# Expert stage of a hybrid transformer layer: gate by tanh, token rows stored already modulated, and the low parts of gate/up weights on VectorE

## The chip, the cores and the metric

The kernel runs on one core of one Trainium2 chip. The metric is device time in microseconds, the median of the runs. The core's engines are TensorE (PE in the profile; PEld is its weight load), VectorE (DVE), ScalarE (ACT), GpSimd (POOL) and SyncE (SP), which issues most of the DMAs. Each engine works through its own list in order, and lists meet only at semaphores.

## What is computed

One layer on 2048 tokens of width 1024, in float32: a mixer (attention and retention), then an expert-choice feed-forward. What matters here is the part behind the mixer:

```python
x = x + ga1 * y                                     # y: mixer output @ w_o
h = rmsnorm(x, g_norm_ffn) * (1.0 + sc2) + sh2
aff = jax.nn.softmax(h @ w_router, axis=-1)         # 16 experts
g, idx = lax.top_k(aff.T, 256)                      # each expert picks 256 tokens
xs = h[idx]
a, u = xs @ w_gate, xs @ w_up                       # 1024 -> 768, per expert
out = (silu(a) * u) @ w_down * g                    # 768 -> 1024
x = x + ga2 * scatter_add(out, idx)
return rmsnorm(x, g_final)
```

## The kernel before

The stages run one behind the other. TensorE multiplies in a fast 32-bit form that keeps fewer bits than float32, so each large operand is split in two: ScalarE rounds it (the high part), VectorE or GpSimd subtract that from the whole (the low part, or "rest"), and three products high x high, high x low, low x high are added up (`PASSES`). The low part overwrites the whole, in place.

**First stage** (`modulation`): the products that give shift and scale. `perm["modcols"]` holds them as columns, columns 24 to 31 the feed-forward's shift, 32 to 39 its scale, into which `g_norm_ffn` is folded last (`s_fold`). At its end SyncE stores one row (`scratch["ga2"]`), waits for that, and goes on to load the first tile of x for the projection stage.

**Output stage** (`mix_out`): one turn per tile m of 128 tokens, 16 turns. TensorE makes the first half of y(m) (24 products of 512 columns), transposes the normed rows of tile m-1 (8 transposes, L1289), makes the second half of y(m), and the router product of m-1 (L1297). VectorE multiplies y by ga1 (L1384), adds x (L1386); ScalarE squares, takes a logarithm and an exponential (L1331 to L1336, each of the two behind a table load), which gives the inverse root; VectorE scales (`xn`, L1392). `xn`, not yet modulated, is stored to `scratch["xn2"]` and transposed. After the transposes VectorE applies scale and shift to the transposed tile, two instructions for each half (L1359, L1361), for the router. GpSimd makes the low parts of the mix tiles (L1269).

**Expert stage** (`experts`): one turn per expert e, 16 turns. TensorE's list of a turn:

- six gate/up pieces f = 0 to 5 (`gate_up`, L1614), 48 products each of 256 columns, 24 for gate and 24 for up; piece f uses the weights of group c = f // 2. Behind f = 1 it makes the slot table of expert e+1.
- two groups of four transposes of e+1's gathered rows (T0 and T1, `transposes`, L1600), into banks 6 and 7.
- twelve down pieces i = 0 to 11 (`down`, L1628), six products of 512 columns each, with T2 behind piece 2 (bank 6 again) and T3 behind piece 3 (bank 7 again).

Each piece f gives a gate in `ex` (ScalarE, Exp), then VectorE's `hidden` in four steps (add 1, reciprocal, two products), ScalarE's rounding and VectorE's low part (L1852). The gathered rows go from the bank by VectorE's `modulate` (L1818 from the bank, L1820 in place), ScalarE's `round_gathered` (L1665) and VectorE's `rest_gathered` (L1826). T2 and T3 wait for `modulated`: the first modulate step of the group two back.

Weights: SyncE loads gate/up group c of e+1 (2 MB) when piece 2c+1 of e is done; down weights come in a ring of six slots (`RING`), 256 KB each, and piece i+6 is loaded when piece i is done. ScalarE rounds them (L1656, L1660). The low part of gate weights is VectorE's (`rest_gate`, L1830), that of up weights GpSimd's (`rest_up`, L1540); down pieces 0 to 5 are VectorE's, 6 to 11 GpSimd's (L1545). GpSimd also issues the gather of rows and the scatter-add of results. ScalarE's list in the second half of a turn is fixed by hand:

```python
                for i, n in ((6, 1), (7, 2), (8, 3)):
                    round_down(e, i)
                    if ahead:
                        round_gathered(e + 1, n)
```

## Time and profile before

| | us |
|---|---|
| median of 3 runs | 3539.58 |
| lowest, highest | 3536.52, 3541.98 |
| the profiled execution: its span | 3526.4 |
| output stage, first to last product of y | 2123.9 to about 2347 |
| expert stage, first gate/up to last down product | 2472.2 to about 3462 |

The page gives the profiled execution by its span alone, from the first to the last instruction; a run's time also holds what lies around that. Times within the kernel are counted from the start of the span. How to read the rows further down: a timeline row has the start, the length and the engine, then line, operation, what is written and read, and how many instructions were merged; in brackets stands how long the engine was idle before it and what released it. A stretch row has the busy time of each engine within it, the granted TensorE clock as a share of 2.4 GHz, and the DMA engines' busy share.

### The profile page before, as it was taken

The numbers are of one execution on the slowest core, as the hardware profiler recorded it, in microseconds if no ns is written. First come the engines' busy times: TensorE is split into PE (matmuls) and PEld (weight loads), VectorE is DVE, ScalarE is ACT, GpSimd is POOL, SyncE is SP. The second block draws the span as 40 slices with busy tenths as digits, with TensorE's granted clock in tenths as the row PEclk, the third lists the DMA queues.
The fourth block names the chain that finished last, engine by engine and source line by source line (L and its number), as shares of the span: only waits on it lengthen the run. The fifth ranks groups of instructions, "written<-read, shape, count | busy, mean of one in ns | idle before, by whom it ended". The sixth has DMA issues, their size and how long they took to land. (4 is left out here: it accounts for less than half of the span.)

```text
span 3526.4 us, 44830 instructions
## 1 busy us (share of the span) xinstructions
PE 3097.0 (88%) x14689; PEld 2192.4 (62%) x14689; DVE 2266.7 (64%) x2823; ACT 1427.3 (40%) x2136; POOL 992.7 (28%) x514
## 2 busy tenths in 40 slices
PE   6899999999786999999999988971988989899892
PEld 1455555555785556556555647850888878888782
DVE  1133333333675777777777764557888989889893
ACT  0133333332223566666556644330334343333433
POOL 0000001100453332332333212211445444444441
PEclk9999999999776999999999999985999999999996
DMA  8412111121322011011001004341565666656656
GB/s 320 149 59 69 59 59 64 66 67 48 102 89 58 4 31 31 5 31 31 23 13 29 5 20 157 125 141 57 156 203 169 191 186 181 196 165 195 190 145 226
DMA packets 252530, 362.92 MB, mean 103 GB/s; under 512 B 34356, under 2 KB 168503, under 8 KB 250808
## 3 DMA queue, kind: packets, MB, share of 16 engines
q1 hardware_dynamic: 243128, 326.91, 28.5%
q0 software_dynamic: 9216, 33.56, 4.3%
q8 instruction: 113, 1.85, 0.2%
q14 instruction: 73, 0.60, 0.1%
HBM read 278.60 MB, written 81.83 MB: 102 GB/s over the span
## 5 line engine op out<-in xcount | busy, mean ns | idle before, releaser
L465 PE MATMUL bank<-w_in_sb,h_T 128*128 128x512 f32 (+1 forms) x1440 | 610.2, 579 | 2.1 <-DVE h_T L614 2.1
L1614 PE MATMUL ebank<-gathered_T,w_gate_up 128*128 128x256 f32 x4608 | 564.9, 284 | 20.5 <-ACT w_gate_up L1656 12.7
L1614 PEld LDWEIGHTS ebank<-gathered_T,w_gate_up 128*128 128x128 f32 x4608 | 560.2, 190 | 24.4 <-issue 23.5
L1075 PE MATMUL abank<-scores,head_v 128*128 128x512 f32 x1152 | 546.0, 602 | 2.2 <-ACT scores L1113 2.2
L1038 PE MATMUL abank<-head_qT,head_kT 96*128 96x512 f32 x1728 | 504.6, 437 | 22.9 <-POOL head_qT L1017 22.9
L465 PEld LDWEIGHTS bank<-w_in_sb,h_T 128*128 128x128 f32 x1440 | 271.1, 191 | 298.9 <-issue 298.7
L1038 PEld LDWEIGHTS abank<-head_qT,head_kT 96*128 96x128 f32 x1728 | 327.7, 190 | 169.9 <-issue 94.7
L1024 POOL TENSOR_TENSOR scores<-scores,max_for_pool 128x1536 f32<-128x1536 f32 x64 | 221.1, 3476 | 570.9 <-ACT max_for_pool L1107 570.9
L1101 ACT ACTIVATE scores<-abank 128x512 f32<-128x512 f32 x576 | 314.2, 608 | 77.0 <-PE abank L1038 71.2
L1075 PEld LDWEIGHTS abank<-scores,head_v 128*128 128x128 f32 x1152 | 218.6, 194 | 180.3 <-issue 162.8
L1628 PE MATMUL ebank<-w_down,hidden_T 128*128 128x512 f32 x1152 | 303.0, 418 | 21.0 <-POOL w_down L1545 20.8
L1540 POOL TENSOR_TENSOR w_gate_up<-w_gate_up_whole,w_gate_up 128x2048 fp32r<-128x2048 f32 x48 | 229.1, 4773 | 268.2 <-ACT w_gate_up L1656 180.0
L1113 ACT ACTIVATE scores<-scores 128x1536 f32<-128x1536 f32 x192 | 287.3, 1498 | 39.8 <-DVE scores L1155 35.5
L1139 DVE TENSOR_TENSOR score_max<-score_max,scores 128x1536 f32<-128x1536 f32 x128 | 225.1, 1758 | 94.4 <-ACT scores L1101 92.9
L1628 PEld LDWEIGHTS ebank<-w_down,hidden_T 128*128 128x128 f32 x1152 | 223.1, 199 | 80.0 <-POOL w_down L1545 30.2
L1155 DVE TENSOR_TENSOR scores<-scores,abank 128x1536 f32<-128x1536 f32 x128 | 218.1, 1744 | 52.0 <-PE abank L1058 52.0
L582 POOL TENSOR_TENSOR q_rope_terms<-q_rows,rope_rows 128x256 f32<-128x256 f32 x18 | 13.0, 724 | 788.1 <-ACT q_rows L552 788.1
L1674 ACT ACTIVATE gate_exp<-ebank 128x256 f32<-128x256 f32 x96 | 36.9, 384 | 453.2 <-DVE hidden_T L1852 237.9
L1280 PE MATMUL obank<-w_o_sb,mix_tile 128*128 128x512 f32 x768 | 184.7, 397 | 20.5 <-DVE w_o_sb L1399 20.5
L1545 POOL TENSOR_TENSOR w_down<-w_down_whole,w_down 128x512 fp32r<-128x512 f32 x96 | 124.0, 1304 | 275.8 <-ACT w_down L1660 275.2
L1656 ACT ACTIVATE w_gate_up<-w_gate_up_whole 128x2048 fp32r<-128x2048 f32 x96 | 176.3, 1900 | 16.6 <-DMA w_gate_up_whole<-in_w_exp_up 16.6
L1280 PEld LDWEIGHTS obank<-w_o_sb,mix_tile 128*128 128x128 f32 x768 | 143.8, 190 | 50.2 <-issue 21.3
(261 smaller groups left out, 4138.3 us busy)
## 6 DMA issues: line engine op xcount, KB each, us to landing
w_gate_up_whole<-in_w_exp_gate SPq DMA_DIRECT2D x48, 1024.0 KB, 5.9
w_gate_up_whole<-in_w_exp_up SPq DMA_DIRECT2D x48, 1024.0 KB, 9.0
w_down_whole<-in_w_exp_down SPq DMA_DIRECT2D x192, 256.0 KB, 2.9
ada_w<-in_w_ada SPq DMA_DIRECT2D x12, 2048.0 KB, 12.8
scratch_ret<-ret_rows SPq DMA_DIRECT2D x72, 256.0 KB, 2.5
x_tile<-in_x_all SPq DMA_DIRECT2D x18, 512.0 KB
w_in_sb<-in_w_in SPq DMA_DIRECT2D x4, 2048.0 KB, 15.0
chunk_qk<-scratch_ret SPq DMA_DIRECT2D x16, 512.0 KB
```

The source lines that it names most:

```text
L465: m = pe.matmul(banks[bank][:, 0:n], hT[u][:, k, :], w_in[:, k, lo:lo + n], start=(k == 0), stop=(k == KD - 1))
L1024: pool.tensor_tensor(x, x, mid(ms[:, :], G), ALU.subtract).then_inc(sg["shifted_pool"].sem, 1)
L1038: m = pe.matmul(banks[kt % 3][:, :], kT[u][:, kp, k], qT[u][:, qp, q], start=(n == 0), stop=(n == 2))
L1075: m = pe.matmul(banks[5 + j % 2][:, :], v1[u][:, kt, :], sc[j % 2][:, kt, :], start=(kt == 0), stop=(kt == T - 1))
L1101: act.activation(sc[j % 2][:, kt, :], banks[kt % 3][:, :], ACT.Copy).then_inc(sg["scores"].sem, 1)
L1113: act.activation(x, x, ACT.Exp, scale=ATT_SCALE).then_inc(sg["probs"].sem, 1)
L1139: dve.tensor_tensor(mx[:, :, :], mx[:, :, :], s[:, g * G:(g + 1) * G, :], ALU.max).then_inc(sg["max_keys"].sem, 1)
L1155: dve.tensor_tensor(x, x, mid(banks[4][:, :], G), ALU.subtract).then_inc(sg["shifted"].sem, 1)
L1280: x = pe.matmul(banks[2 * u + half][:, :], mt[u][:, mp, k, :], w_o[:, wp, k, half * 512:(half + 1) * 512], start=(k == 0 and n == 0), stop ...
L1540: pool.tensor_tensor(w_gu[c][:, 1, 1], w_gu_whole[c][:, 1, 1], w_gu[c][:, 0, 1].bitcast(F32), ALU.subtract).then_inc(sg["up_rest"].sem, 1)
L1614: x = pe.matmul(banks[f % 3][:, j * CAP:(j + 1) * CAP], w_gu[c][:, wp, j, k, o:o + P], xsT[:, xp, k, :], start=(k == 0 and n == 0), stop=( ...
L1628: x = pe.matmul(banks[Y_BANKS[2 * c + h]][:, :], hid[:, hp, k, h * P:(h + 1) * P], w_d[i % RING][:, wp, :], start=(k == 0 and n == 0), sto ...
```

## The change

1. The first stage also stores shift and scale as one row of 2048 numbers to `scratch["ffn_rows"]`, and the output stage loads that row to all partitions (`ffn_rows`, 1 MB).
2. The output stage applies them before the rows are stored: `xs = x2 * inverse root * scale`, then `xn = xs + shift`. So `scratch["xn2"]` holds modulated rows. The transposed tile for the router is only copied.
3. In the expert stage `modulate` is gone. ScalarE rounds the gathered rows straight from the bank and VectorE subtracts from the bank. T2 and T3 wait for `gathered_rest`, the subtraction two groups back.
4. The gate: ScalarE computes tanh(a/2), and `hidden` is two steps, (t + 1) * a and then * 0.5 * u, since silu(a) = 0.5 * a * (1 + tanh(a/2)).
5. The low parts of up weights move from GpSimd to VectorE (`rest_gate_up`); GpSimd keeps those of down pieces 6 to 11.

ScalarE's list keeps its order, and so do SyncE's loads within the expert stage.

```diff
@@ modulation, SyncE
             sp.dma_start(scratch["ga2"], ga2[0:1, :]).then_inc(s_ga2, 16)
+            sp.wait_ge(s_fold, 5)
+            sp.dma_start(scratch["ffn_rows"].rearrange("o (j p) -> p (o j)", p=P), perm["modcols"][:, 0, 24:40], allow_slow_non_contiguous=True).then_inc(perm["ffn_rows_stored"], 16)
             sp.wait_ge(s_ga2, 16)
@@ mix_out, SyncE
             load(CTX + P, 1)
+            sp.wait_ge(perm["ffn_rows_stored"], 16)
+            sp.dma_start(ffn_rows[:, :, :].rearrange("p j d -> p (j d)"), scratch["ffn_rows"].partition_broadcast(P)).then_inc(r_loaded, 16)
@@ mix_out, VectorE, router(m)
-                    dve.tensor_tensor(o, banks[4 + g][:, :].rearrange("p (k n) -> p k n", k=4), last(perm["modcols"][:, 0, 32 + 4 * g:36 + 4 * g], P), ALU.mult).then_inc(sg["h2T"].sem, 1)
-                    sg["h2T"].wait(dve, m, 2 * g + 1)
-                    dve.tensor_tensor(o, o, last(perm["modcols"][:, 0, 24 + 4 * g:28 + 4 * g], P), ALU.add).then_inc(sg["h2T"].sem, 1)
+                    dve.tensor_copy(h2T[:, 4 * g:4 * g + 4, :].rearrange("p k n -> p (k n)"), banks[4 + g][:, :]).then_inc(sg["h2T"].sem, 1)
@@ mix_out, VectorE, turn
-                dve.tensor_scalar(xn[:, :], x2[u][:, :], st[:, 1:2], None, ALU.mult).then_inc(sg["x2_normed"].sem, 1)
+                if first:
+                    dve.wait_ge(r_loaded, 32)
+                dve.scalar_tensor_tensor(xs[:, :], x2[u][:, :], st[:, 1:2], ffn_rows[:, 1, :], ALU.mult, ALU.mult).then_inc(sg["x2_scaled"].sem, 1)
+                sg["x2_scaled"].wait(dve, m)
+                settled(dve)
+                dve.tensor_tensor(xn[:, :], xs[:, :], ffn_rows[:, 0, :], ALU.add).then_inc(sg["x2_normed"].sem, 1)
@@ experts, TensorE, transposes(e, n)
-                sg["modulated"].wait(pe, e, 2 * (n - 2) + 1)
+                sg["gathered_rest"].wait(pe, e, n - 1)
@@ experts, TensorE, gate_up(e, f)
-                sg["gate_rest"].wait(pe, e, c + 1)
-                sg["up_rest"].wait(pe, e, c + 1)
+                sg["gu_rest"].wait(pe, e, 2 * c + 2)
@@ experts, ScalarE
-                sg["modulated"].wait(act, e, 2 * n + 2)
-                act.activation(xsT[:, 0, 4 * g:4 * g + 4, h * P:(h + 1) * P], xm[n % 2][:, :, :], ACT.Copy).then_inc(sg["gathered_rounded"].sem, 1)
+                sg["xT_psum"].wait(act, e, n + 1)
+                sg["gu_psum"].wait(act, e - 1)
+                act.activation(xsT[:, 0, 4 * g:4 * g + 4, h * P:(h + 1) * P], banks[6 + n % 2][:, :].rearrange("p (k n) -> p k n", k=4), ACT.Copy).then_inc(sg["gathered_rounded"].sem, 1)
...
-                act.activation(ex[f % 2][:, :], banks[f % 3][:, 0:CAP], ACT.Exp, scale=-1.0).then_inc(sg["gate_exp"].sem, 1)
+                act.activation(ex[f % 2][:, :], banks[f % 3][:, 0:CAP], ACT.Tanh, scale=0.5).then_inc(sg["gate_exp"].sem, 1)
@@ experts, VectorE, hidden(e, f)
-                dve.tensor_scalar(x[:, :], x[:, :], 1.0, None, ALU.add).then_inc(s.sem, 1)
-                s.wait(dve, e, 4 * f + 1)
-                dve.reciprocal(x[:, :], x[:, :]).then_inc(s.sem, 1)
-                s.wait(dve, e, 4 * f + 2)
-                dve.tensor_tensor(x[:, :], banks[f % 3][:, 0:CAP], x[:, :], ALU.mult).then_inc(s.sem, 1)
-                s.wait(dve, e, 4 * f + 3)
+                dve.scalar_tensor_tensor(x[:, :], x[:, :], 1.0, banks[f % 3][:, 0:CAP], ALU.add, ALU.mult).then_inc(s.sem, 1)
+                s.wait(dve, e, 2 * f + 1)
                 sg["d_psum"].wait(dve, e - 1)
-                dve.tensor_tensor(x[:, :], banks[f % 3][:, CAP:], x[:, :], ALU.mult).then_inc(s.sem, 1)
+                dve.scalar_tensor_tensor(x[:, :], x[:, :], 0.5, banks[f % 3][:, CAP:], ALU.mult, ALU.mult).then_inc(s.sem, 1)
```

How the order of instructions changes, at three places. First VectorE in the output stage, one turn near the end; before:

```order
L1386 TENSOR_TENSOR x_tile<-x_tile,x_again 128x1024
L1366 TENSOR_REDUCE router_stats<-obank 128x1
L1392 TENSOR_SCALAR x_normed<-x_tile,x_stats 128x1024
L1371 RECIPROCAL router_stats<-router_stats 128x1
L1373 TENSOR_SCALAR affinities<-router_exp,router_stats 128x16
L1359 TENSOR_TENSOR h_T<-obank,mod_cols 128x512
L1361 TENSOR_TENSOR h_T<-h_T,mod_cols 128x512
L1359 TENSOR_TENSOR h_T<-obank,mod_cols 128x512
L1361 TENSOR_TENSOR h_T<-h_T,mod_cols 128x512
```

and now:

```order
L1389 TENSOR_TENSOR x_tile<-x_tile,x_again 128x1024
L1369 TENSOR_REDUCE router_stats<-obank 128x1
L1397 SCALAR_TENSOR_TENSOR x_scaled<-x_tile,x_stats,ffn_rows 128x1024
L1400 TENSOR_TENSOR x_normed<-x_scaled,ffn_rows 128x1024
L1374 RECIPROCAL router_stats<-router_stats 128x1
L1376 TENSOR_SCALAR affinities<-router_exp,router_stats 128x16
L1364 COPY h_T<-obank 128x512 x2
```

One scaling became two steps over 1024 columns, and four steps on the transposed tile became two copies behind them.

Second VectorE in the expert stage, from `hidden(5)` to the first steps of y; before (the last low part of a hidden piece stands between two modulate pairs):

```order
L1852 TENSOR_TENSOR hidden_T<-gate_exp,hidden_T 128x256
L1818 TENSOR_TENSOR modulated<-ebank,mod_cols 128x512
L1820 TENSOR_TENSOR modulated<-modulated,mod_cols 128x512
L1852 TENSOR_TENSOR hidden_T<-gate_exp,hidden_T 128x256
L1818 TENSOR_TENSOR modulated<-ebank,mod_cols 128x512
L1820 TENSOR_TENSOR modulated<-modulated,mod_cols 128x512
L1826 TENSOR_TENSOR gathered_T<-modulated,gathered_T 128x4x128
L1818 TENSOR_TENSOR modulated<-ebank,mod_cols 128x512
L1820 TENSOR_TENSOR modulated<-modulated,mod_cols 128x512
L1826 TENSOR_TENSOR gathered_T<-modulated,gathered_T 128x4x128
```

and now, from `hidden(5)`'s low part of piece 4 on, up to the weights of group 1:

```order
L1835 TENSOR_TENSOR hidden_T<-gate_exp,hidden_T 128x256
L1812 TENSOR_TENSOR gathered_T<-ebank,gathered_T 128x4x128
L1835 TENSOR_TENSOR hidden_T<-gate_exp,hidden_T 128x256
L1812 TENSOR_TENSOR gathered_T<-ebank,gathered_T 128x4x128 x3
L1841 SCALAR_TENSOR_TENSOR expert_out<-ebank,slot_gates,ga_again 128x512 x4
L1817 TENSOR_TENSOR w_gate_up<-w_gate_up_whole,w_gate_up 128x2048 x2
```

The eight modulate steps are gone, and the low part of a gathered group reads the bank; the weights' row counts two steps where one stood.

Third ScalarE at the same place, gate 5 to the rounding of down weights 7; before:

```order
L1674 ACTIVATE gate_exp<-ebank 128x256
L1669 ACTIVATE hidden_T<-gate_exp 128x256
L1665 ACTIVATE gathered_T<-modulated 128x4x128
L1669 ACTIVATE hidden_T<-gate_exp 128x256
L1660 ACTIVATE w_down<-w_down_whole 128x512
L1665 ACTIVATE gathered_T<-modulated 128x4x128
L1660 ACTIVATE w_down<-w_down_whole 128x512
```

and now:

```order
L1671 ACTIVATE gate_exp<-ebank 128x256
L1666 ACTIVATE hidden_T<-gate_exp 128x256
L1662 ACTIVATE gathered_T<-ebank 128x4x128
L1666 ACTIVATE hidden_T<-gate_exp 128x256
L1656 ACTIVATE w_down<-w_down_whole 128x512
L1662 ACTIVATE gathered_T<-ebank 128x4x128
L1656 ACTIVATE w_down<-w_down_whole 128x512
```

Nothing moved here: the rounding of down weights 6 still stands ahead of the rounding of gathered group 1. Only the source changed, from `modulated` to a bank.

## Rows read from the trace of the kernel before

**Rows 1.** Stretch table, core 0: microseconds, each engine's busy time (instructions), granted clock, DMA share, GB/s.

```profile
2205.50:2219.50 14.00, 13.79 (x74) 11.54 (x73) 7.32 (x11) 5.62 (x10) 3.00 (x2) 1.00 0.38 131
...
2905.00:2967.00 62.00, 56.78 (x411) 51.73 (x411) 54.62 (x77) 24.30 (x35) 29.17 (x14) 0.97 0.63 189
```

**Rows 2.** TensorE timeline, one expert turn: start, length, line, operation [idle before, releaser].

```profile
3033.56 11.68 PE L1614 MATMUL ebank<-gathered_T,w_gate_up 128*128 128x256 f32 x96
...
3069.07 1.04 PE L1600 MATMUL ebank<-ident,gathered 128*128 128x128 f32 x8
...
3078.39 1.11 PE L1600 MATMUL ebank<-ident,gathered 128*128 128x128 f32 x4 [4.08 <-DVE modulated L1818]
3079.15 2.91 PE L1628 MATMUL ebank<-w_down,hidden_T 128*128 128x512 f32 x6
...
3098.24 13.20 PE L1614 MATMUL ebank<-gathered_T,w_gate_up 128*128 128x256 f32 x96 [2.52 <-ACT w_gate_up L1656]
```

**Rows 3.** TensorE timeline, a quicker expert turn, around the third group of transposes.

```profile
2640.69 0.66 PE L1600 MATMUL ebank<-ident,gathered 128*128 128x128 f32 x4 [1.73 <-DVE modulated L1818]
2641.10 1.64 PE L1628 MATMUL ebank<-w_down,hidden_T 128*128 128x512 f32 x6
```

**Rows 4.** TensorE timeline, start of the first turn, its first transposes, start of the last.

```profile
2472.22 13.79 PE L1614 MATMUL ebank<-gathered_T,w_gate_up 128*128 128x256 f32 x96 [5.54 <-DVE gathered_T L1826]
...
2509.86 1.03 PE L1600 MATMUL ebank<-ident,gathered 128*128 128x128 f32 x8
...
3410.01 34.72 PE L1614 MATMUL ebank<-gathered_T,w_gate_up 128*128 128x256 f32 x288
```

**Rows 5.** TensorE timeline, output stage: router product, then transposes.

```profile
2206.79 1.86 PE L1297 MATMUL obank<-w_router_sb,h_T 128*128 128x16 f32 x16
...
2214.41 1.09 PE L1289 MATMUL obank<-ident,x_normed 128*128 128x128 f32 x8 [0.20 <-DVE x_normed L1392]
```

**Rows 6.** VectorE timeline, output stage: addition of x, then the scaling.

```profile
2207.72 1.23 DVE L1386 TENSOR_TENSOR x_tile<-x_tile,x_again 128x1024 f32<-128x1024 f32 x1
...
2213.52 0.75 DVE L1392 TENSOR_SCALAR x_normed<-x_tile,x_stats 128x1024 f32<-128x1024 f32 x1 [4.49 <-ACT x_stats L1336]
```

**Rows 7.** Instruction groups by shape, expert stage, VectorE: busy us, mean ns, idle before.

```profile
L1843 DVE RECIPROCAL gate_exp<-gate_exp 128x256 f32<-128x256 f32 x96 | 168.3, 1753 | 3.3
...
L1820 DVE TENSOR_TENSOR modulated<-modulated,mod_cols 128x512 f32<-128x512 f32 x60 | 75.8, 1263 | 2.1
...
L1826 DVE TENSOR_TENSOR gathered_T<-modulated,gathered_T 128x512 fp32r<-128x512 f32 x60 | 45.4, 757 | 1.5
```

**Rows 8.** One tile, w_gate_up_whole: duration in ns, shortest/median/longest, by instruction.

```profile
L1540 POOL TENSOR_TENSOR w_gate_up<-w_gate_up_whole,w_gate_up x48: 4497/4599/6468, 2380.3 to 3424.7; 128x2048 fp32r<-128x2048 f32 x48
L1830 DVE TENSOR_TENSOR w_gate_up<-w_gate_up_whole,w_gate_up x48: 2276/2283/6704, 2452.9 to 3419.4; 128x2048 fp32r<-128x2048 f32 x48
```

**Rows 9.** ScalarE timeline, quicker turn: rounding of down weights 6.

```profile
2643.23 0.63 ACT L1660 ACTIVATE w_down<-w_down_whole 128x512 fp32r<-128x512 f32 x1 [0.90 <-DMA w_down_whole<-in_w_exp_down]
```

**Rows 10.** DMA issues in 2636.3 to 2637.1 us: count, KB, us to landing.

```profile
w_down_whole<-in_w_exp_down SPq DMA_DIRECT2D x1, 256.0 KB, 6.8
```

**Rows 11.** Stretch table after a hole of 1.97 us.

```profile
3270.00:3272.00 2.00, 2.00 (x7) 1.42 (x6) 1.72 (x3) 0.85 (x2) 0.70 (x1) 0.50 0.66 243
```

**Rows 12.** One line, L1981, the final norm on VectorE: shortest/median/longest ns.

```profile
L1981 DVE SCALAR_TENSOR_TENSOR final_out<-final_in,final_stats,g_final_rows x16: 1276/1280/1286, 3496.3 to 3521.7; 128x1024 f32<-128x1024 f32 x16
```

**Rows 13.** SyncE's queue timeline, end of the first stage.

```profile
119.59 0.26 SPq L228 DMA_DIRECT2D scratch_ga<-ga_rows  x1
```

**Rows 14.** ScalarE timeline, first square of the projection stage.

```profile
124.69 1.06 ACT L525 ACTIVATE square_out<-x_tile 128x1024 f32<-128x1024 f32 x1 [101.81 <-DMA x_tile<-in_x_all]
```

**Rows 15.** DMA packets in 1517 to 1519 us.

```profile
DMA packets 1028, 0.39 MB, mean 193 GB/s; under 512 B 1012, under 2 KB 1012, under 8 KB 1012
```

**Rows 16.** Instruction groups by shape, output stage, GpSimd.

```profile
L1269 POOL TENSOR_TENSOR mix_tile<-ret_mix_T,mix_tile 128x512 fp32r<-128x512 f32 x14 | 24.4, 1745 | 0.0
```

**Rows 17.** VectorE timeline: a step that started beside one of GpSimd's.

```profile
2938.88 4.66 DVE L1852 TENSOR_TENSOR hidden_T<-gate_exp,hidden_T 128x256 fp32r<-128x256 f32 x1
```

78 lines of the change are left out of this document (27 added, 51 removed).

## The prediction

> **What bounds the kernel now.** I read the stretch table first, then TensorE's timeline, then who releases it. The diff touches two stages and a corner of a third. In the output stage (2124 to 2363 us; one turn per 128 tokens) TensorE is busy 13.79 of 14.00 us; in the expert stage (2472 to 3461 us; sixteen turns) it is busy 56.78 of 62 us and VectorE 54.62 [rows 1]. TensorE is the bound in both, so a shorter VectorE list is worth only the holes that it leaves in TensorE.
>
> An expert turn has two halves. From its first gate/up product to the first transposes, the moment G, it takes 3069.07 - 3033.56 = 35.5 us without a hole. From G to the next turn there are the four groups of transposes T0 to T3 and twelve down pieces. In the turn shown, T2 (the third group) waits 4.08 us for VectorE's modulate, and the next turn begins 2.52 us late, on ScalarE; the second half is 3098.24 - 3069.07 = 29.2 us [rows 2]. In a quicker turn T2 waits 1.73 us [rows 3]. The fifteen turns with a successor last 3410.01 - 2472.22 = 937.8 us, 62.5 each [rows 4].
>
> In the output stage the loop is a chain: second half of y done, VectorE multiplies and adds, ScalarE makes the inverse root, VectorE scales (0.75 us), TensorE transposes, second half of y of the next tile. TensorE waits there 0.20 us [rows 5]; VectorE itself waits 4.49 us for ScalarE just before the scaling, so nothing of its own can be moved forward [rows 6]. The chain has no slack to speak of.
>
> **Expert stage, the VectorE list.** Per expert it loses six reciprocals of 1.75 us and, for the four modulate pairs, an addition of 1.26 us each [rows 7]; it gains three low parts of weights from GpSimd, 2.28 us each by the median (up to 6.70 where it had to stand back for GpSimd's, which take 4.60) [rows 8]. So -10.5 - 5.1 + 6.8 = -8.8 us on these alone, with fewer small steps on top. GpSimd loses 3 x 4.6 us. None of this is on the path by itself; it makes VectorE early. Gate/up pieces wait for `hidden` two pieces back and for all low parts of their weights: with the new order one_hot, hidden(0) and four 2.28 us low parts end at about 16 us of the turn, hidden(0) at 10.6, needed at 12.4. Cover 1.8 us; no wait there.
>
> **Where the wait goes.** This is the step on which the result hangs. T2 reuses the bank of T0 and T3 that of T1. Until now T2 and T3 needed only VectorE's first multiplication; now they need ScalarE's rounding and VectorE's subtraction of the same bank (`gathered_rest`). For T2 that is early: gate(5) at G+0.4, two 0.4 to 0.6 us steps, then 0.69; done by G+2.5, while T2 comes up at G+5.2. For T3 it isn't: ScalarE's list has round_down(6) ahead of round_gathered(1), and that waits for down weights 6, whose load is issued at G+2.6 (after piece 0 frees its slot) behind 2 MB of gate/up weights, and lands 6.6 to 6.8 us later: G+9.3. In the quicker turn of today ScalarE starts it at 2643.23 = G+9.5, having waited 0.90 us for the transfer [rows 9, 10]. Then 0.55 (round), 0.63 (round gathered), 0.76 (subtraction, [rows 7]) and handovers: T3 starts at G+11.45. TensorE comes to it at G+7.3. The wait of some 4 us is not removed but passed from VectorE's list to the queue ScalarE - DMA - ScalarE - VectorE.
>
> After T3 nothing more is late: pieces 6 to 11 come at G+14.6 and later, their low parts on GpSimd are ready at G+11.5, 12.9, 14 and then 4.8 us after each slot frees, against 7 us of cover; next gate/up weights 1 are rounded by G+24. So the second half is 11.45 + 0.42 + 8 x 1.41 = 23.15 us.
>
> Low clock: after the 4.08 us hole T2 took 1.11 and the next piece 2.91 us, against 0.66 and 1.64 in the turn with the 1.73 us hole [rows 2, 3]. That is 1.7 us, and a little in the pieces behind: 1.9. Bounds 0.9 and 2.5. Where a hole of 1.97 us had been, a stretch shows the granted clock at 0.50, which is 1.2 of the 2.4 GHz [rows 11]; so even a shorter hole can do it. Second half: 25.05 us (24.0 to 25.7).
>
> Fifteen turns: 15 x (35.5 + 25.05) = 908, and the first one starts at the low clock, 37.6 us instead of 35.5 [rows 4]: 910.4, so **-27.4 us**. Ahead of the first turn four modulations (4 x 1.4 us in a row on VectorE) fall out of the chain gather, transposes, rounding; against them two more low parts stand before the gather lands, in time: **-3.9**, between -2 and -5. Expert stage **-31**, between -48 and -18.
>
> **Output stage.** The scaling becomes a scalar_tensor_tensor of 128x1024 and an addition of 128x1024 behind a wait on it. Nearest rows: 1.28 us for the first form and 1.23 for the second, in place of 0.75 [rows 6, 12]; with 0.04 for the handover +1.80 us. It stands in the chain, in fifteen loop turns: 27, and in the last tile +1.8 less 1.2 for two copies in place of four steps. The two copies themselves (0.69 each) end long before the router product. **+27.6**; from 24 (if each is worth 1.6) to 30.
>
> The 1.95 us hole that each tile then has may bring the low clock. In the expert stage it followed three of the eleven holes between 1.5 and 2.8 us; one of them cost 13.20 - 11.68 = 1.5 us in the next 96 products [rows 2], so about 1.6. Here transposes, which keep TensorE little busy, follow at once; I take one in three. 15 x 1/3 x 1.6 = **+8**, bounds 0 and 24.
>
> **Start.** The store of the two rows takes 128 x 16 single elements and stands ahead of the first x_tile load, on which ScalarE waits (it starts at 124.69 [rows 14]; the store follows the one issued at 119.59 [rows 13]). No row has such elements. The nearest is a load of 256 B packets: 1012 of them in 2 us at full DMA share, 2 x 16 / 1012 = 0.032 us each on an engine [rows 15]. 128 per engine: 4 us, of which 1.3 lie in the time until the load arrives: **+3**; lower bound 0.5 (overlapped), upper 8 (twice that price). The Trainium skill, DMA: Bandwidth & Descriptors, Rules for kernel authors, says that a strided last dimension becomes one descriptor per element; no run here shows it yet. The 1 MB load of the rows in the output stage lands some 10 us before its first use; nothing.
>
> Sum: -31 + 27.6 + 8 + 3 = **+7.6 us**, span 3534. The page shows only a span, 3526.4 us; the median of the three runs, 3539.6, is 13.2 above it (what lies around the span, and the difference between executions). 3539.6 + 7.6 = **3547 us**.
>
> **Rivals.** (a) *T3 doesn't wait.* If weights 6 were there early, the second half would be 0.84 + 0.84 + 12 x 1.41 = 18.6 us and a turn 54.1: 15 x 8.4 = 126 us less, plus 3.9: 3540 - 130 + 27.6 + 8 + 3 = 3448. Against it: the transfer landed between 6.5 and 7.5 us in all fifteen turns, and the list on ScalarE is the same. Chance 0.07.
>
> (b) *The output chain hides the addition.* If the 1.8 us fell into something that I take for chain, the sum loses 27.6 and 8: 3511. For it only that the last tiles showed no hole; against it 0.20 us and the 4.49 us wait on ScalarE. 0.10, which includes smaller gains of both stages.
>
> (c) *Slower: GpSimd takes the port between the two new steps.* The new steps read two SBUF tensors each, as does GpSimd's low part of the mix tile (mean 1.75 us [rows 16]); in the expert stage such a step of only 256 columns took 4.66 us beside one of GpSimd's [rows 17]. GpSimd's comes about 0.9 us after the scaling starts; now both new steps are under way then, so it can get in between. Price 1.5 us a tile, 15 x 1.5 = 22: 3569. It decides when the mix tile is rounded before the first new step ends. The Trainium skill, GPSIMD Engine Reference, Specifications, says that GpSimd's SBUF interfaces are shared with VectorE, with contention for instructions with two SBUF inputs. The trace agrees for the low parts (4.66 us). Chance 0.15.
>
> (d) My forecast 0.65; rest 0.03.
>
> **How the numbers follow.** Around 3547 the own bounds give 3530 to 3565. The range takes in most of (c) and the near part of (b): 3520 to 3569. A measurement of this kernel can tell about 0.2%, 7 us. Faster than 3532.5: 0.07 + 0.10 and 0.06 of my own case, 0.23. Within: 0.30, nearly all mine. Slower than 3546.7: 0.15, and 0.32 of mine, 0.47.
>
> **What would show it.** In TensorE's timeline of the expert stage: no wait before T2, about 4 us before T3, released by VectorE's subtraction, which waited for ScalarE, which waited for a w_down transfer; no waits on GpSimd's low parts; turns of 60 to 61 us, all alike. In the output stage: about 2 us before the transposes and tiles of 15.8 us. At the start: the first ScalarE square near 128. I'm wrong if T3 doesn't wait (turns of 54), if output tiles stay at 14, or if the clock in the output stage stays at 1.00 (then 3539) or falls in each tile (3563).

## The result, and the profile after

The changed kernel takes 3561.8 us (median of four runs, 3554.0 to 3563.0) against 3539.6 for the kernel before: ratio 1.0052, 95% interval 1.004 to 1.0064. It is **slower by 22 us**. The forecast was 3547, slower as the likeliest sign (0.47), with 3520 to 3569 as the range.

The profiled execution has a span of 3560.5 us, 34.1 more than that of before. Cut at the first instruction of each stage (first square on ScalarE, then the first TensorE instruction of each stage), the two traces differ so:

| stretch, us | before | after | difference |
|---|---|---|---|
| up to the first square | 124.7 | 133.5 | +8.8 |
| projection | 767.2 | 767.3 | +0.2 |
| retention | 218.6 | 226.1 | +7.5 |
| attention | 1013.5 | 1013.1 | -0.4 |
| output stage | 242.1 | 287.4 | **+45.3** |
| search, up to the first transposes T0 | 96.3 | 89.7 | -6.6 |
| T0 to the first gate/up product | 10.0 | 6.3 | -3.8 |
| fifteen expert turns | 937.8 | 921.5 | **-16.3** |
| the rest | 116.4 | 115.6 | -0.8 |

**Expert stage.** TensorE's timeline of one turn of after, from G (the first transposes of a turn, here 2620.71; S, further down, is a turn's start) to the next turn; columns as in [rows 2]:

```profile
2620.71 1.03 PE L1597 MATMUL ebank<-ident,gathered 128*128 128x128 f32 x8
...
2625.80 0.60 PE L1597 MATMUL ebank<-ident,gathered 128*128 128x128 f32 x4
...
2631.92 1.12 PE L1597 MATMUL ebank<-ident,gathered 128*128 128x128 f32 x4 [4.12 <-DVE gathered_T L1812]
2632.69 13.30 PE L1624 MATMUL ebank<-w_down,hidden_T 128*128 128x512 f32 x48
2647.29 0.97 PE L1610 MATMUL ebank<-gathered_T,w_gate_up 128*128 128x256 f32 x6 [1.30 <-ACT w_gate_up L1652]
```

T2 (2625.80) doesn't wait any more, where it waited 4.08 us in [rows 2]. T3 (2631.92) waits 4.12 us, at G+11.2, and after it the clock is low (granted 0.85 in these pieces): 1.12 us for the transposes, 13.30 for eight down pieces that take 11.49 at the full clock (a row further down). ScalarE's timeline of the same turn has the cause, the rounding of down weights 6 and behind it that of the second gathered group; then VectorE's, the subtraction that releases T3:

```profile
2630.03 0.63 ACT L1656 ACTIVATE w_down<-w_down_whole 128x512 fp32r<-128x512 f32 x1 [7.30 <-DMA w_down_whole<-in_w_exp_down]
2630.56 0.58 ACT L1662 ACTIVATE gathered_T<-ebank 128x512 fp32r<-128x512 f32 x1
```

```profile
2631.17 0.69 DVE L1812 TENSOR_TENSOR gathered_T<-ebank,gathered_T 128x512 fp32r<-128x512 f32 x1 [7.62 <-ACT gathered_T L1662]
```

ScalarE sits 7.30 us in front of a weight that hasn't landed, with a rounding behind it whose operand has been there since G+1. The waits of TensorE in the whole stage (total, times, longest) are these:

```profile
PE ebank L1597 <- DVE gathered_T L1812: 67.4, 15, 5.9
PE ebank L1610 <- ACT w_gate_up L1652: 5.2, 4, 1.5
PE ebank L1610 <- issue: 3.4, 2, 1.9
```

In the kernel before, the transposes' waits and those of the down pieces on GpSimd's low parts (the last number, 20.8 us) were these:

```profile
PE ebank L1600 <- DVE modulated L1818: 51.3, 21, 4.3
L1628 PE MATMUL ebank<-w_down,hidden_T 128*128 128x512 f32 x1152 | 303.0, 418 | 21.0 <-POOL w_down L1545 20.8
```

The waits on GpSimd's low parts are gone. What is left beside T3 are six holes at the start of every second turn, 8.6 us in all. They are taken up below.

**Output stage.** VectorE's two new steps, GpSimd's nearest step, and TensorE in two tiles:

```profile
2228.07 1.28 DVE L1397 SCALAR_TENSOR_TENSOR x_scaled<-x_tile,x_stats,ffn_rows 128x1024 f32<-128x1024 f32 x1 [4.59 <-ACT x_stats L1342]
2229.51 1.23 DVE L1400 TENSOR_TENSOR x_normed<-x_scaled,ffn_rows 128x1024 f32<-128x1024 f32 x1 [0.15 <-DVE x_scaled L1397]
```

```profile
2230.22 1.66 POOL L1275 TENSOR_TENSOR mix_tile<-mix_tile_whole,mix_tile 128x512 fp32r<-128x512 f32 x1 [14.76 <-ACT mix_tile L1328]
```

```profile
2230.79 1.10 PE L1295 MATMUL obank<-ident,x_normed 128*128 128x128 f32 x8 [2.14 <-DVE x_normed L1400]
2231.64 5.74 PE L1286 MATMUL obank<-w_o_sb,mix_tile 128*128 128x512 f32 x24
...
2246.75 1.19 PE L1295 MATMUL obank<-ident,x_normed 128*128 128x128 f32 x8 [2.12 <-DVE x_normed L1400]
2247.59 7.32 PE L1286 MATMUL obank<-w_o_sb,mix_tile 128*128 128x512 f32 x24
```

The hole before the transposes is 2.1 us, against 0.20 in [rows 5]. The first half of y behind it takes 5.74 us in one tile and 7.32 in the next. The stretch table for the first two tiles (length, busy times, then the granted clock) shows why: the tile of 15.95 us has the clock at 1.00, that of 17.55 has 0.90.

```profile
2230.80:2246.75 15.95, 13.83 (x73) 11.56 (x73) 7.34 (x11) 5.62 (x10) 2.83 (x3) 1.00 0.33 115
2246.75:2264.30 17.55, 15.41 (x73) 12.75 (x73) 7.32 (x10) 5.62 (x10) 2.68 (x3) 0.90 0.30 105
```

Of the twelve tiles from 2179.8 to 2383.9 us, eight take 17.5 us and four 15.95, always two slow ones behind a quicker one; before, a tile takes 14.04.

**Start.** ScalarE's first square (it stood at 124.69 in [rows 14]), the store's landing time, and the DMA packets of 120 to 132 us with the queue's share of 16 engines:

```profile
133.49 1.06 ACT L527 ACTIVATE square_out<-x_tile 128x1024 f32<-128x1024 f32 x1 [110.84 <-DMA x_tile<-in_x_all]
```

```profile
scratch_ffn_rows<-mod_cols SPq DMA_DIRECT2D x1, 8.0 KB, 11.7
```

```profile
DMA packets 2178, 0.45 MB, mean 37 GB/s; under 512 B 2069, under 2 KB 2069, under 8 KB 2178
q1 hardware_dynamic: 2178, 0.45, 81.5%
```

**Search.** Two rows of VectorE before that are not among those shown: small steps of the search, which take 0.21 and 0.83 us where GpSimd is idle. GpSimd's first low parts begin at 2380.3 us [rows 8].

```profile
2380.81 4.06 DVE L1723 TENSOR_TENSOR search_candidates<-threshold,search_steps 128x48 uint32<-128x48 uint32 x1 [0.39 <-DVE search_steps L1736]
...
2387.66 3.80 DVE L1735 COPY_PREDICATED threshold<-search_keep,search_candidates 128x16 uint32<-128x16 uint32 x3
```

In after GpSimd has no low parts there, and the two groups' means fall from 483 to 208 ns and from 246 to 179 ns.

### The profile page after: what moved, and what is told of

Its sections match the earlier page's. It is cut to its first block and busy times, and to the rows that moved or that the text cites. A ratio compares the mean times of both kernels' runs of the same rounds, so it can differ in the third digit from the quotient of the medians.

```text
span 3560.5 us, 44128 instructions
## 1 busy us (share of the span) xinstructions
PE 3111.9 (87%) x14689; PEld 2210.6 (62%) x14689; DVE 1914.2 (54%) x2535; ACT 1424.7 (40%) x2136; POOL 750.3 (21%) x466
## 5 line engine op out<-in xcount | busy, mean ns | idle before, releaser
L1610 PEld LDWEIGHTS ebank<-gathered_T,w_gate_up 128*128 128x128 f32 x4608 | 557.1, 189 | 14.0 <-issue 13.2
L1115 ACT ACTIVATE scores<-scores 128x1536 f32<-128x1536 f32 x192 | 287.4, 1498 | 40.2 <-DVE scores L1157 38.0
L1624 PEld LDWEIGHTS ebank<-w_down,hidden_T 128*128 128x128 f32 x1152 | 232.1, 205 | 54.5
L1817 DVE TENSOR_TENSOR w_gate_up<-w_gate_up_whole,w_gate_up 128x2048 fp32r<-128x2048 f32 x96 | 215.3, 2285 | 13.5 <-ACT w_gate_up L1652 13.4
L1286 PE MATMUL obank<-w_o_sb,mix_tile 128*128 128x512 f32 x768 | 196.0, 414 | 20.2 <-DVE w_o_sb L1407 20.2
L1656 ACT ACTIVATE w_down<-w_down_whole 128x512 fp32r<-128x512 f32 x192 | 113.5, 624 | 204.5 <-DMA w_down_whole<-in_w_exp_down 204.5
L1286 PEld LDWEIGHTS obank<-w_o_sb,mix_tile 128*128 128x128 f32 x768 | 152.6, 202 | 52.7 <-issue 21.0
L1652 ACT ACTIVATE w_gate_up<-w_gate_up_whole 128x2048 fp32r<-128x2048 f32 x96 | 176.3, 1900 | 16.3 <-DMA w_gate_up_whole<-in_w_exp_up 16.3
(256 smaller groups left out, 3464.5 us busy)
```

Source lines behind the costliest of these rows:

```text
L1115: act.activation(x, x, ACT.Exp, scale=ATT_SCALE).then_inc(sg["probs"].sem, 1)
L1286: x = pe.matmul(banks[2 * u + half][:, :], mt[u][:, mp, k, :], w_o[:, wp, k, half * 512:(half + 1) * 512], start=(k == 0 and n == 0), stop ...
L1610: x = pe.matmul(banks[f % 3][:, j * CAP:(j + 1) * CAP], w_gu[c][:, wp, j, k, o:o + P], xsT[:, xp, k, :], start=(k == 0 and n == 0), stop=( ...
L1624: x = pe.matmul(banks[Y_BANKS[2 * c + h]][:, :], hid[:, hp, k, h * P:(h + 1) * P], w_d[i % RING][:, wp, :], start=(k == 0 and n == 0), sto ...
L1817: dve.tensor_tensor(w_gu[c][:, 1, j], w_gu_whole[c][:, 1, j], w_gu[c][:, 0, j].bitcast(F32), ALU.subtract).then_inc(sg["gu_rest"].sem, 1)
```

## The experiments

Each was timed beside the kernel before, on the same chip. The three series of four (the rows from t3_first to gate_and_low, from third_load_later to four_mends, and the last four) ran on three chips, with medians of before of 3540.2, 3545.7 and 3543.1 us, so a difference between runs of two series is known to a few us only; the ratios and the traces go beside it where it matters.

| kernel | us | ratio to before, 95% interval | mean expert turn | output stage |
|---|---|---|---|---|
| before | 3539.6 | | 62.5 | 242.1 |
| changed | 3561.8 | 1.0052 (1.004 to 1.0064) | 61.4 | 287.4 |
| t3_first | 3506.0 | 0.9904 (0.9888 to 0.9921) | 57.6 | 287.5 |
| product_ahead | 3528.6 | 0.9967 (0.9956 to 0.9979) | 61.3 | 253.0 |
| store_late | 3556.2 | 1.0045 (1.0029 to 1.006) | 61.4 | 287.6 |
| gate_and_low | 3464.5 | 0.9784 (0.9768 to 0.9801) | 58.4 | 242.0 |
| third_load_later | 3501.8 | 0.9874 (0.985 to 0.9898) | 57.3 | 289.8 |
| gate_low_load | 3450.2 | 0.9733 (0.9708 to 0.9758) | 57.4 | 241.1 |
| gate_alone | 3475.4 | 0.9799 (0.9774 to 0.9823) | 58.3 | 242.1 |
| four_mends | 3449.8 | 0.9724 (0.9696 to 0.9751) | 56.8 | 253.1 |
| four_pe4 | 3421.2 | 0.9658 (0.9628 to 0.9688) | 55.1 | 253.4 |
| four_pe16 | 3408.8 | 0.963 (0.9598 to 0.9662) | 54.2 | 253.4 |
| low_pe16 | 3405.6 | 0.9617 (0.9585 to 0.9649) | 54.4 | 242.3 |
| before_pe16 | 3530.8 | 0.9969 (0.9955 to 0.9983) | 62.1 | 242.3 |

### T3's wait: t3_first and third_load_later

The first moves one rounding in ScalarE's list:

```diff
+                if ahead:
+                    round_gathered(e + 1, 1)
-                for i, n in ((6, 1), (7, 2), (8, 3)):
+                for i, n in ((6, 2), (7, 3), (8, None)):
                     round_down(e, i)
-                    if ahead:
+                    if ahead and n:
                         round_gathered(e + 1, n)
```

> The changed kernel with one line moved: on ScalarE the rounding of the second gathered group stands ahead of the rounding of down weights 6 (the third and fourth follow down weights 6 and 7). Theory (T3 waits in ScalarE's queue for a weight transfer): the fifteen waits before T3, 67.4 us in the trace of the changed kernel, go, and with them 1.5 to 1.9 us of low clock each, 25 us; piece 6 of the down product now comes at G+10.5, before its own low part (weights landed G+9.3, 0.6 rounding, 1.3 on GpSimd, G+11.4), and waits 0.9 us, 13 us in all. 3562 - 67 - 25 + 13 = 3483. Rival 1 (VectorE's own list holds T3, ScalarE only seems to): T3 still waits 2 us or more, 3530 or above. Rival 2 (the load of the down weights bounds the whole half, the wait moves from T3 to piece 6 one for one): 3555 to 3562, with waits of 4 us at piece 6.

ScalarE's rounding of down weights 6 and TensorE's timeline in the same turn (G is 2617.72, T3 is the first of TensorE's rows):

```profile
2627.18 0.63 ACT L1656 ACTIVATE w_down<-w_down_whole 128x512 fp32r<-128x512 f32 x1 [6.95 <-DMA w_down_whole<-in_w_exp_down]
```

```profile
2624.64 0.60 PE L1597 MATMUL ebank<-ident,gathered 128*128 128x128 f32 x4
...
2629.22 8.69 PE L1624 MATMUL ebank<-w_down,hidden_T 128*128 128x512 f32 x36 [1.18 <-POOL w_down L1548]
```

T3 (2624.64) comes at G+6.9 without a wait; piece 6 waits 1.18 us for its low part on GpSimd. This is the theory's picture, and both rivals fall. The gain is 56 us, not 79. The turns were to be 56 us and are 57.6: piece 6 waits 2.2 to 2.7 us in five turns (23.7 us in fifteen turns, for 13 expected), with a low clock behind it in four of them (10.0 to 10.2 us for these 36 products instead of 8.69), and a hole at every second turn's start has grown from 1.2 to 1.9 us to as much as 3.0 (in one turn it is only 0.3).

The second leaves ScalarE's list and takes the 2 MB away that stood ahead of down weights 6:

```diff
-                    for c in range(NG):
+                    for c in range(NG - 1):
                         sg["gu_psum"].wait(sp, e, 2 * c + 2)
...
                     load_down(e, i) if i < ND else load_down(e + 1, i - ND)
+                    if ahead and i == ND - 1:
+                        sg["gu_psum"].wait(sp, e)
+                        settled(sp)
+                        load_gate_up(e + 1, NG - 1)
```

> The changed kernel with one load moved in SyncE's list: the third quarter-megabyte-times-eight of the next expert's gate/up weights (2 MB) is issued behind down weights 11 instead of ahead of down weights 6. ScalarE's list stays as in the changed kernel (down weights 6 before the second gathered group). Theory (T3 waits for ScalarE, which waits for down weights 6, which wait in the DMA queue behind 2 MB; the queue moved 350 to 385 GB/s there, so those 2 MB are some 5 us): without them down weights 6, issued at G+2.6, land by G+5.1, T3's operand is ready at G+7.1, when T3 comes up: the 67 us of waits and 25 us of low clock go, and piece 6 doesn't wait either, since its low part is there at G+7. 3562 - 92 = 3470. Rival (ScalarE's order alone is the cause, the landing has a latency of its own of 5 us or more): T3 still waits 2 us or more, 3520 to 3540. Rival (the moved 2 MB come late for the next turn, or hold its down weights): a new wait at the start of the turn or at the first down pieces, 3550 or above.

ScalarE's rounding of down weights 6, then TensorE from T3 to the next turn (G is 2620.72):

```profile
2625.92 0.63 ACT L1660 ACTIVATE w_down<-w_down_whole 128x512 fp32r<-128x512 f32 x1 [3.18 <-DMA w_down_whole<-in_w_exp_down]
```

```profile
2627.81 0.66 PE L1601 MATMUL ebank<-ident,gathered 128*128 128x128 f32 x4
2628.23 11.49 PE L1628 MATMUL ebank<-w_down,hidden_T 128*128 128x512 f32 x48
2643.47 6.74 PE L1614 MATMUL ebank<-gathered_T,w_gate_up 128*128 128x256 f32 x34 [3.75 <-DVE w_gate_up L1821]
```

Down weights 6 are rounded at 2625.92, which is G+5.2 instead of G+9.3. T3 has no wait in fourteen of fifteen turns, and none of the down pieces waits. So the wait was the sum of the two: an order on ScalarE and a queue of 2 MB in front of the weight, and either can be taken away. But 60 us were gained where 92 were expected. In the last row TensorE stands 3.75 us at the start of a turn, again at every second one, six holes of 3.8 to 4.7 us, each with a slower first half behind it (S to G 36.9 to 38.3 us instead of 35.5; granted clock 0.80 in the first 13.5 us behind the hole shown). So the first rival falls. Of the second, a longer hole at the start of turns is there, but not the time of 3550.

### The output chain: product_ahead

```diff
+                sg["x2"].wait(dve, m)
+                settled(dve)
+                dve.tensor_tensor(xs[:, :], x2[u][:, :], ffn_rows[:, 1, :], ALU.mult).then_inc(sg["x2_scaled"].sem, 1)
+                sg["x2_scaled"].wait(dve, m)
                 sg["x2_rstd"].wait(dve, m)
...
-                dve.scalar_tensor_tensor(xs[:, :], x2[u][:, :], st[:, 1:2], ffn_rows[:, 1, :], ALU.mult, ALU.mult).then_inc(sg["x2_scaled"].sem, 1)
-                sg["x2_scaled"].wait(dve, m)
                 settled(dve)
-                dve.tensor_tensor(xn[:, :], xs[:, :], ffn_rows[:, 0, :], ALU.add).then_inc(sg["x2_normed"].sem, 1)
+                dve.scalar_tensor_tensor(xn[:, :], xs[:, :], st[:, 1:2], ffn_rows[:, 0, :], ALU.mult, ALU.add).then_inc(sg["x2_normed"].sem, 1)
```

> The changed kernel with the product by the first modulation row taken before ScalarE's inverse root is there: x2 times the row while VectorE waits for ScalarE (4.5 us in the trace), and behind the wait a single instruction, times the root plus the second row (a form of 1.28 us). The arithmetic is the same up to the order of the two factors. Theory (the two steps lengthen a chain that has no slack): the chain is 0.5 us longer than in the kernel before instead of 1.95, so 15 x 1.4 = 21 us less than the changed kernel, and 5 to 8 us of low clock as well: 3562 - 28 = 3534, tiles of 14.6 us. Rival (the output stage became longer for something else, the two copies in place of four steps or the traffic of the rows): tiles stay at 15.9 and the time at 3560.

VectorE's product and the step behind the wait, then TensorE's transposes and first half of y:

```profile
2201.95 1.23 DVE L1396 TENSOR_TENSOR x_scaled<-x_tile,ffn_rows 128x1024 f32<-128x1024 f32 x1
2206.53 1.28 DVE L1402 SCALAR_TENSOR_TENSOR x_normed<-x_scaled,x_stats,ffn_rows 128x1024 f32<-128x1024 f32 x1 [3.35 <-ACT x_stats L1342]
```

```profile
2207.95 1.09 PE L1295 MATMUL obank<-ident,x_normed 128*128 128x128 f32 x8 [0.89 <-DVE x_normed L1402]
2208.79 5.73 PE L1286 MATMUL obank<-w_o_sb,mix_tile 128*128 128x512 f32 x24
```

The product fills 1.23 us of VectorE's wait for ScalarE (3.35 us of it are left), one step stands behind it, the hole is 0.89 us, and the tiles from 2178.5 to 2355.1 us take 14.7 each. No y half is slow. 33 us were gained for 28 expected. The stage is 253.0 us, so 34 of its 45 us are gone: of these the chain explains 15 x 1.25 = 19 (the hole went from 2.14 to 0.89), and some 15 are the low clock, which here came behind holes of 2.1 us and not behind those of 0.9. The rival falls.

### The start: store_late

```diff
-            sp.wait_ge(s_fold, 5)
-            sp.dma_start(scratch["ffn_rows"].rearrange("o (j p) -> p (o j)", p=P), perm["modcols"][:, 0, 24:40], allow_slow_non_contiguous=True).then_inc(perm["ffn_rows_stored"], 16)
...
             load_x(P, 1)
+            sp.dma_start(scratch["ffn_rows"].rearrange("o (j p) -> p (o j)", p=P), perm["modcols"][:, 0, 24:40], allow_slow_non_contiguous=True).then_inc(perm["ffn_rows_stored"], 16)
```

> The changed kernel with the store of the two modulation rows (2048 single elements) issued behind the first two x tiles and the last weights of the projection instead of ahead of them. Theory (the store held the first x tile back by 8.8 us, and the projection's transfers have room): first ScalarE square at 124.7 us instead of 133.5, 3562 - 9 = 3553. Rival 1 (only the 3 us that I predicted are the store's, the rest is between executions): first square at 130 and 3559. Rival 2 (the elements cost the same wherever they stand, since the next loads queue behind them): the first square is early, but the second or third tile is held, and the time stays at 3562.

ScalarE's timeline:

```profile
124.80 1.06 ACT L526 ACTIVATE square_out<-x_tile 128x1024 f32<-128x1024 f32 x1 [102.10 <-DMA x_tile<-in_x_all]
```

The first square is back at 124.80 us, 8.7 earlier. The median falls by 5.6 us, which with runs from 3550.0 to 3562.7 is barely told from 9; the spans differ by 6.1. The projection is 1.6 us longer, and retention 0.9. Rival 1 falls. A small part of rival 2 may be true.

### The parts of the change: gate_alone and gate_and_low

Both start from the kernel before. The first takes over `hidden` and `gate_exp` of the diff (tanh, two VectorE steps for four), the second also `rest_gate_up` in place of `rest_gate` and GpSimd's `rest_up`.

> The kernel before with the gate by tanh alone: per expert six reciprocals and twelve other small steps of VectorE become twelve steps; low parts and modulation stay. Theory (T2 waited because VectorE was late, by 10.5 us of reciprocals per turn): T2's and T3's waits (51 us in all in the kernel before) go, with about 15 to 20 us of low clock; the waits for GpSimd's low parts (21 us) stay or grow a little: 3540 - 51 - 17 = 3472, up to 3485. Rival (the low parts' contention on VectorE made it late, the reciprocals lie in VectorE's idle time): 3520 to 3540.

> The kernel before with two of the three parts of the change: the gate by tanh, and the low parts of gate/up weights on VectorE. Rows are stored and gathered as before and modulated in the expert stage, so start and output stage are those of before. Theory (T3's new wait comes only from the part that makes ScalarE read the transposes, and the wait at T2 came from VectorE's lateness): T2 and T3 need only the first step of a modulation, done at G+2.7 and G+4.5, before they come up at G+5.1 and G+6.9; neither waits; piece 6 waits about 0.9 us for its low part. A turn of 35.5 + 19.6 and on average 0.6 for the loop's end: 55.7 against 62.5: 3540 - 15 x 6.8 = 3438, up to 3460 where holes of 1 to 2 us are left. Rival (VectorE, with the modulations kept, is still late for T2 by 1 to 2 us): 3490 to 3510. Rival (the gain of the expert stage came from the rows stored modulated): 3540, no change.

TensorE's timeline of a turn of gate_alone, with T2, T3 and piece 6 (G is 2692.00):

```profile
2697.08 0.60 PE L1600 MATMUL ebank<-ident,gathered 128*128 128x128 f32 x4
...
2698.91 0.60 PE L1600 MATMUL ebank<-ident,gathered 128*128 128x128 f32 x4
...
2703.52 9.91 PE L1628 MATMUL ebank<-w_down,hidden_T 128*128 128x512 f32 x36 [1.21 <-POOL w_down L1545]
```

Neither T2 nor T3 waits. The tanh gate alone gains 70 us and makes the turn 58.3 us. The low parts' move leaves the turn at 58.4 and takes 6.7 us off the search (96.7 to 90.0 us up to T0), where GpSimd's low parts had held VectorE up; the rivals of both runs fall. And so the third part, the rows stored modulated, costs 3561.8 - 3464.5 = **97 us** (95 by the ratios): in the traces +8.0 at the start, +45 in the output stage, -3.7 between T0 and the first product, +46 in fifteen turns (58.4 to 61.4), in sum +96.

gate_and_low was to be at 3438 to 3460 and is at 3464.5. One reason is the hole at every second turn's start, 2.5 to 2.8 us, with a slower first half (37.0 us for 35.5) behind three of the six. The other is GpSimd. Its six low parts of a turn, first in gate_alone, then in t3_first:

```profile
2702.20 9.35 POOL L1545 TENSOR_TENSOR w_down<-w_down_whole,w_down 128x512 fp32r<-128x512 f32 x6 [12.16 <-ACT w_down L1660]
```

```profile
2627.90 7.55 POOL L1548 TENSOR_TENSOR w_down<-w_down_whole,w_down 128x512 fp32r<-128x512 f32 x6 [26.01 <-ACT w_down L1656]
```

In gate_alone and gate_and_low VectorE still has modulate steps and the low parts of the gathered rows at this time, and each of GpSimd's steps takes 1.56 us instead of 1.26, longer than a down piece (1.41). VectorE's subtractions beside them are slower too, 1.34 to 1.75 us for 0.68; that the one slows the other is argued from this overlap. So pieces 7 to 10 wait some 0.3 us each as well, and the 36 products from piece 6 on take 9.9 us in nearly every turn, where t3_first needs 8.69. The granted clock is 1.00 in both stretches, so this is not the clock.

### Both together: gate_low_load and four_mends

gate_low_load is gate_and_low with the load moved as in third_load_later; four_mends is the changed kernel with t3_first, product_ahead, store_late and third_load_later in one.

> The kernel before with the gate by tanh, the low parts on VectorE, and the load of the third gate/up weights moved as in the run above. Theory: against the run with gate and low parts alone (3464.5, turns of 58.4 us, of which piece 6 waits 1.1 to 1.4 us for its low part in every turn, and at low clock behind it) the wait at piece 6 goes: turns of 35.5 + 18.6 and 1.1 for the loop's end on average, 55.2: 3464.5 - 15 x 3.2 = 3417. Rival (with the load later another wait of the same size comes in its place): 3455 to 3465.

> The changed kernel with all four edits: second gathered group ahead of down weights 6 on ScalarE, the product ahead of the inverse root, the store of the rows late, and the third gate/up load behind down weights 11. Theory (the effects are in different stages or, the first and the last, remove the same wait in two ways): 3562 - 92 (expert stage) - 33 (output stage, measured) - 6 (start, measured) = 3431, with expert turns of 55.2 us. Rival (they are not additive, since an earlier expert stage or start meets the DMA): 3450 or above.

Both are too slow against their expectations, four_mends by 19 us and gate_low_load by 33. The rival of gate_low_load, another wait of the same size in place of the one removed, is half true: the holes at the turns' starts went from 2.5 to 2.8 us to 5.0, but the time fell by 14. four_mends lies on the edge of its rival's 3450. Its stages do add up, though: 69 us in the turns, 34 in the output stage and 9 at the start make the 112 between 3561.8 and 3449.8. It is the 92 for the expert stage that was too much. In gate_low_load the waits inside the turns are gone but for three short ones, 2 us in all. Each second turn starts behind a hole of 5.0 us, and its way to G takes 37.3 to 37.6 us instead of 35.5:

```profile
2567.49 11.54 PE L1621 MATMUL ebank<-w_down,hidden_T 128*128 128x512 f32 x48
2584.02 3.35 PE L1607 MATMUL ebank<-gathered_T,w_gate_up 128*128 128x256 f32 x14 [5.00 <-issue]
```

The theory for these runs had 1.1 us a turn for this. What makes the hole? The trace names ScalarE, VectorE, GpSimd or "issue" for it, in one kernel now this and now that. It stands only where the loop of two turns jumps back, and the last two whole turns, behind which there is no jump, take 54.5 and 54.6 us in gate_low_load and 54.04 in four_mends. And one thing is alike in all of them: the DMA's instruction queue starts a transfer of 16 KB some 2.8 to 3.2 us before the first product behind a jump, in each of the 41 holes of seven kernels that I compared (before, changed, t3_first, gate_and_low, third_load_later, gate_low_load, four_mends; holes of 1.1 to 5.2 us). The one hole of 0.3 us in t3_first has it too. For the hole above it is in the 0.3 us from 2580.9, 3.0 us before 2584.02 (packets, MB, share of 16 engines):

```profile
q1 hardware_dynamic: 58, 0.11, 98.2%
q8 instruction: 1, 0.02, 23.0%
```

### The loop's end: four_pe4, four_pe16, low_pe16, before_pe16

```diff
-            loop(pe, turn)
+            for e in range(E):
+                turn(e, e % 2, int(e < E - 1))
```

That is four_pe16, low_pe16 and before_pe16, from four_mends, gate_low_load and before. four_pe4 has iterations of four turns. Only TensorE's list is touched.

> The kernel of the four edits (3449.8 us), with TensorE's expert loop written as iterations of four turns and four turns behind it, instead of two and two: three jumps back instead of six. Nothing else changes. Theory (the hole of 4.0 to 4.8 us at every second turn's start is the loop's end: after the jump TensorE's instructions are fetched anew by a transfer, and the last two turns, without a jump between them, take 54.04 us against 57.3 on average): each jump costs 3.7 to 4.8 us and 1.6 to 2.6 of low clock, 6.5 in all: 3449.8 - 3 x 6.5 = 3430, holes only at every fourth turn. Rival (the hole is a wait for the next expert's weights or rows that the trace puts down wrongly): the same six holes, 3450.

> The same kernel with TensorE's sixteen turns written out, no jump. Theory: all six holes go, 3449.8 - 6 x 6.5 = 3411, turns of 54.0 to 54.6 us. Rival (code without a loop has to be fetched all along, and the transfers compete with the weights): holes in other places, 3430 or above. Rival (a wait for weights): 3450.

> The kernel before with gate by tanh, low parts on VectorE and the third load later (3450.2 us), with TensorE's sixteen turns written out. Theory: six holes of 5.0 us and 1.6 to 2.1 of low clock behind each go, 6 x 6.9 = 41: 3409, the same as the kernel with the modulated rows and four edits, so the rows bring nothing in the end. Rival (the modulated rows are worth something once the holes are gone, since VectorE is less busy): this one stays above the other by 10 us or more.

> The kernel before with only TensorE's sixteen turns written out. Theory: its six holes at every second turn's start (2.25 to 2.74 us, 15 in all) go, with some low clock behind one or two of them: 3540 - 15 to 20 = 3522. Rival (VectorE, which is late at T2, bounds these turns, and TensorE that comes earlier waits longer there): 3535 to 3540.

I had miscounted in the first: seven iterations of two turns have six jumps, and three of four turns have two, not three. So four holes go, and two are in the trace, at 2706 and 2930 us; 3449.8 - 3421.2 = 28.6, or 7.2 for each. Without a jump 41.0 us go, 6.8 for each (by the traces' turns, 852.3 to 812.9 us, 6.6). A turn of four_pe16 (TensorE's timeline; the rows left out have no idle time either):

```profile
2638.94 11.67 PE L1615 MATMUL ebank<-gathered_T,w_gate_up 128*128 128x256 f32 x96
...
2674.40 1.03 PE L1602 MATMUL ebank<-ident,gathered 128*128 128x128 f32 x8
...
2681.32 0.60 PE L1602 MATMUL ebank<-ident,gathered 128*128 128x128 f32 x4
2681.67 11.47 PE L1629 MATMUL ebank<-w_down,hidden_T 128*128 128x512 f32 x48
2692.98 2.20 PE L1615 MATMUL ebank<-gathered_T,w_gate_up 128*128 128x256 f32 x17
```

2692.98 - 2638.94 = 54.04 us, and fourteen of the fifteen turns have exactly this length. The hole was no wait for weights, and code written out has no price here. Between 2585 and 2693 us the instruction queue has six transfers of 16 KB (for which engine, it doesn't say), but TensorE doesn't stand still for any of them, so the rival of the code that has to be fetched all along falls by its holes and by the time. low_pe16 comes to 3405.6, 137 us under the kernel before in its series, the same as four_pe16's 3408.8 within the intervals; its rival falls. With the holes gone, the modulated rows are worth nothing: 7 us less from T0 to the end of the fifteen turns, 11 us more in the output stage.

In the kernel before the same edit gains only 12 us. Its six holes of 15 us in all are gone, but the waits at the transposes have grown from 51.3 to 63.6 us:

```profile
PE ebank L1600 <- DVE modulated L1819: 63.6, 16, 5.1
```

There VectorE's lateness set the time, and TensorE mostly waited at another place: the fifteen turns became only 5.9 us shorter. The result lies between the theory's 3522 and the rival's 3535 to 3540.

## Why the prediction was right or wrong, point by point

- **What bounds it.** TensorE, with a floor under its turns: 54.1 us was computed in rival (a), and four_pe16 shows 54.04.
- **T2's wait goes, T3's comes.** Right, and in size: T3 at G+11.2 for 11.45, 4.1 to 4.3 us in twelve turns (5.3 to 5.9 in three), behind ScalarE, behind a transfer. Undoing either link of the chain removed it. Low clock: 1.9 us predicted; in the turn shown 0.5 in the transposes and 1.8 in the pieces, 2.3, and over the fifteen turns 1.5 to 2.5, 1.9 in the mean.
- **The second half of the turn, 25.05 us: this step failed.** It is 24.6 in turns without a jump, and 26.6 to 28.1 in those with one. I had put the late start of a turn down to ScalarE, as the trace names it [rows 2], and then dropped it from the sum as if it went with the rest. It is the loop's end: six holes, 8.6 us, in the changed kernel. With the three longer waits of T3 (4 us), less some 2 because T3 came 0.1 to 0.2 us earlier than G+11.45 in the other twelve, this is the difference between -27.4 and -16.3. The term for the start of the stage, -3.9, measured -3.8; the search's -6.6 was not foreseen, since I looked at GpSimd's low parts in the turns [rows 8] and not at what they did to VectorE before the first turn.
- **Output stage, 27.6 + 8.** The chain is right: the hole grew by 1.93 for 1.80. The low clock's price of 1.6 us is right, its frequency was wrong: two tiles in three for one in three, 8 too little. The stage took 45.3 for 35.6.
- **Start, 3 us, at most 8.** Measured 8.8. The term was mis-sized because the price per packet came from a load of 256 B packets [rows 15]; 2178 packets took 81.5% of twelve us on 16 engines, 0.072 us each, and the store needed 11.7 us to land. Of the Trainium skill, DMA: Bandwidth & Descriptors, Rules for kernel authors, this is borne out: one descriptor per element, 2048 elements among 2069 packets under 512 B.
- **From the span to the median, 13.2 us.** What lies around the span is 1.8 to 1.9 us in every run but one (2.5). The rest was this: the profiled execution of before was some 11 us quicker than its median. The retention stage, which no edit touches, took 217.7 to 227.4 us in the fourteen traces, 218.6 in that of before and 226.1 in that of after, with the granted clock at 0.84 and 0.67 in the same part of it (1040 to 1060 us before, 1050 to 1071 after):

```profile
1040.00:1060.00 20.00, 16.47 (x123) 15.82 (x122) 14.34 (x17) 6.13 (x12) 10.75 (x10) 0.84 0.25 79
```

```profile
1049.70:1070.70 21.00, 18.09 (x107) 17.34 (x106) 14.20 (x17) 6.12 (x12) 10.60 (x10) 0.67 0.22 74
```

  So 7.5 of the 34 us between the spans belong to no part of the change. The stages leave 27, and the medians differ by 22; for these last 4 or 5 us no run has the reason.
- **The rivals.** (a) was the wrong picture for this change, but a true one of what the other order gives. (b): the chain hid nothing. (c): GpSimd's step starts at 2230.22 us, behind the start of the second new step (2229.51), and both new steps have the duration of a free VectorE, 1.28 and 1.23 us; it didn't get in between, for the mix tile is rounded only later. The 0.9 us that (c) went by was a misreading: in the trace of before, too, GpSimd's step starts 1.9 to 2.9 us behind the start of the scaling. The contention itself is real: in the search it cost 6.6 us, and the overlap in gate_alone looks like more of it.
- **The sum.** +7.6 was made of -31 and +38.6; by the stages of the two traces, without retention, it is -27 and +54. The errors in the output stage, at the start and in the turns add up to 27, and the search took 6.6 of them back, which was luck, since I had not looked there: 20. By the medians the time came out 15 above the forecast, nearer only by the unexplained part between spans and medians. So the sign and the two chains were foreseen, and the loss was put too small in the output stage and at the start, and the gain too large in the turns.

## What to carry to other kernels

Take a change apart before judging it: here two parts gained 75 us and the third lost 97, half of it by hanging a reader of the transposes behind a wait for a weight on an in-order engine. An operation moved into a chain without slack costs its length in each turn, and more by the low clock that the hole brings; do what doesn't need the late operand ahead of the wait. And where a hole comes back at each n-th turn, compare its place with the loop's jump before believing the engine that the profile names.
